# Second attention: half of its output normed and turned inside the loop, and gate products issued a step ahead

## The reference

```python
def diff_attention(q, k, v, lam):               # 8 heads, each with 2 maps of 64 channels
    ...
        s = jnp.einsum('bqhmd,bkhmd->bhmqk', qblk, k) * (HEAD_DIM ** -0.5)
        p = jax.nn.softmax(s, axis=-1)
        p = p[:, :, 0] - lam * p[:, :, 1]
        return jnp.einsum('bhqk,bkhe->bqhe', p, v)
    ...
def token_mixer(h, ...):
    z_hy, q, k, v, gates = jnp.split(h @ w_in, SPLITS, axis=-1)
    y_hy = hyena_branch(...) @ w_hy_out
    ...                                          # 256 own keys and 256 context keys
    o = diff_attention(q, k, v, lam)
    o = rmsnorm_2(o, subln_g) * (1.0 - lam_init) # over the 128 channels of one head
    y_da = o.reshape(B, L, D_ATTN) @ w_da_out
    g_hy, g_da = jnp.split(jax.nn.sigmoid(gates), 2, axis=-1)
    return (g_hy * y_hy + g_da * y_da) @ w_o
```

## Time and profile before

| | |
|---|---|
| median of 3 runs | 2538.65 us |
| profiled execution, its own time | 2539.34 us |
| its span (first to last instruction) | 2537.5 us |
| PE busy | 2464.7 us, 97% |
| DVE busy | 1777.1 us, 70% |
| ACT busy | 1448.3 us, 57% |
| chain that ended last | PE 89%, DVE 6%, ACT 2%, issue 1%, DMA 1% |
| the attention loop with its tail | 2194.27 to 2302.31 us from the span's start |

### The profile page before, as it was taken

The page is one execution under the profiler, slowest core; times in us unless marked ns, Lnnn a source line. Parts: engine busy times, 40 slices in busy tenths (PEclk is TensorE's granted clock), DMA queues, the critical chain, the costliest instruction groups (busy, mean ns, idle before and its releaser), DMA issues.

```text
span 2537.5 us, 32448 instructions
## 1 busy us (share of the span) xinstructions
PE 2464.7 (97%) x11675; PEld 1970.2 (78%) x11675; DVE 1777.1 (70%) x1662; ACT 1448.3 (57%) x1571; POOL 92.8 (4%) x76
## 2 busy tenths in 40 slices
PE   8999999989999999999999999999999999998999
PEld 6578887667788888888888887888884697677887
DVE  6464546668888898889888986655443578777554
ACT  4454344456777777777777775445442344466443
POOL 0000000012000000000000000410000000000000
PEclk9899999999999999999999999999999999998999
DMA  6867663768999999999999997665543354335651
GB/s 222 288 232 239 213 213 108 265 222 310 390 394 374 390 371 387 368 394 367 390 374 382 372 350 269 230 203 182 182 165 108 113 171 150 123 98 176 213 186 66
DMA packets 333407, 650.29 MB, mean 256 GB/s; under 512 B 14856, under 2 KB 113736, under 8 KB 333128
## 3 DMA queue, kind: packets, MB, share of 16 engines
q1 hardware_dynamic: 327992, 630.73, 70.5%
q0 software_dynamic: 5232, 18.38, 1.8%
q10 hardware_dynamic: 96, 0.02, 0.0%
HBM read 634.91 MB, written 14.17 MB: 256 GB/s over the span
## 4 chain that ended last, share of the span: by engine, by line
PE 89%; DVE 6%; ACT 2%; issue 1%; DMA 1%; SPq 0%; POOL 0%; DVEq 0%; ACTq 0%; POOLq 0%
PE ps L961 23%; PE ps L874 20%; PE ps L1001 11%; PE ps L916 10%; PE ps L806 5%; PE ps L1355 5%; PE ps L1385 2%; PE ps L1287 2%; DVE ringL L2424 1%; PE ps L1092 1%; PE ps L986 1%; PE ps L849 1%; PE ps L887 1%; PE ps L1504 1%; DVE As L2454 1%
## 5 line engine op out<-in xcount | busy, mean ns | idle before, releaser
L2454 DVE TENSOR_TENSOR As<-ringA,As 128x2048 fp32r<-128x2048 f32 x316 | 728.5, 2306 | 205.8 <-ACT As L1714 108.2
L961 PE MATMUL ps<-As,xgs 128*128 128x512 f32 x2688 | 648.6, 394 | 8.2 <-DVE As L2454 5.9
L961 PEld LDWEIGHTS ps<-As,xgs 128*128 128x128 f32 x2688 | 501.8, 189 | 113.5 <-issue 6.2
L1803 ACT ACTIVATE As<-ringA 128x2048 fp32r<-128x2048 f32 x224 | 429.0, 1915 | 100.1 <-PE ps L961 94.9
L874 PE MATMUL ps<-As,xs 128*128 128x512 f32 x1408 | 363.2, 395 | 0.0
L1001 PE MATMUL ps<-Bs,hds 128*128 128x512 f32 x1320 | 318.5, 390 | 1.8 <-DVE hds L2525 1.4
L874 PEld LDWEIGHTS ps<-As,xs 128*128 128x128 f32 x1408 | 262.0, 188 | 56.4
L1001 PEld LDWEIGHTS ps<-Bs,hds 128*128 128x128 f32 x1320 | 247.0, 188 | 55.5 <-issue 4.3
L2544 DVE TENSOR_TENSOR Bs<-ringB,Bs 128x2048 fp32r<-128x2048 f32 x110 | 251.8, 2289 | 18.1 <-ACT Bs L1842 17.8
L916 PE MATMUL ps<-Bs,hds 128*128 128x512 f32 x1056 | 248.0, 390 | 0.1
L1842 ACT ACTIVATE Bs<-ringB 128x2048 fp32r<-128x2048 f32 x110 | 211.4, 1922 | 59.0 <-PE ps L1001 58.1
(11 more groups left out here) (436 smaller groups left out, 3185.7 us busy)
## 6 DMA issues: line engine op xcount, KB each, us to landing
ringB<-in_moe_w_down SPq DMA_DIRECT2D x112, 1024.0 KB, 7.3
ringA<-in_moe_w_gate SPq DMA_DIRECT2D x112, 1024.0 KB, 7.4
ringA<-in_moe_w_up SPq DMA_DIRECT2D x112, 1024.0 KB, 7.0
ringA<-in_w_ff_in SPq DMA_DIRECT2D x132, 512.0 KB, 4.6
ringA<-in_w_in SPq DMA_DIRECT2D x56, 1024.0 KB, 5.3
ringA<-in_w_ada SPq DMA_DIRECT2D x36, 1024.0 KB, 6.9
ringB<-in_w_ff_out SPq DMA_DIRECT2D x33, 1024.0 KB, 4.9
ringA<-in_dense_w_gate SPq DMA_DIRECT2D x28, 512.0 KB, 3.5
```

The lines of the kernel that those rows point to most:

```text
L961: m = mm(ps[:, bank, :], lhs(l, tt, k), As[:, h, r, k % 4, :], start=k == 0 and n == 0, stop=k == KC - 1 and n == 2)
L1803: A(As[:, h, 0, :, :], ringA[:, (p["a"] + u) % 2, 4 * h:4 * h + 4, :], ACT.Copy).then_inc(A_high, 1)
L2454: V.tensor_tensor(As[:, h, 1, :, :], ringA[:, (p["a"] + u) % 2, 4 * h:4 * h + 4, :], f32(As[:, h, 0, :, :]), ALU.subtract).then_inc(A_spli ...
```

## The change

Nothing is added to or taken from the arithmetic on PE. Six things move.

1. PE issues `gates_part(0)` ahead of the loop and `gates_part(n + 1)` at the head of step n. The splits of the gates' weights on ACT and DVE stay in their steps, but for one ACT copy ahead of the loop (second half of block 0), which now stands among the copies of the turned q and k.
2. Norm of heads 0 to 3 in the loop: two table loads and a small square root on ACT in step 9, a reciprocal and two scalings of 512 columns on DVE at the end of step 10 (`heads_scaled(0)`).
3. `turn_out` of heads 0 to 3 goes into PE's step 14, to banks 4 and 5; their split stands behind the loop on DVE and in step 15 on ACT.
4. DVE's `weight_low` for the first half of "dao" moves from behind the loop to the end of step 14, ahead of the softmax arithmetic of step 15.
5. Heads 4 to 7 are normed, and then turned by PE between the first and the second of the products of block 0.
6. On DVE the `weight_low` of the second half of "dao" goes ahead of the split of heads 4 to 7.

```diff
+            def turn_out(src, at, hf):
+                for tt in range(TILES):
+                    if at == 0:
+                        pe.wait_ge(o_scaled, 2 * hf + tt + 1)
+                    ...
             scores(0)
             scores(1)
+            gates_part(0)
             for n in range(NU):
                 h = n // 2
-                gates_part(n)
+                if n + 1 < NU:
+                    gates_part(n + 1)
                 pe.wait_ge(s2_p, n + 1)
...
                 if n + 2 < NU:
                     scores(n + 2)
+                elif n + 2 == NU:
+                    turn_out(O2, 0, 0)
                 pe.wait_ge(s2_pt, n + 1)
...
-            pe.wait_ge(s2_o, NU)
-            pe.wait_ge(pj_act, ph["gt2"]["ja"] + 8)
-            for hf in range(2):
-                turn_out(O2, 0, hf)
             p = ph["dao"]
...
                     for tt in range(TILES):
+                        if n == 0 and h == 0 and tt == 1:
+                            pe.wait_ge(s2_o, NU)
+                            pe.wait_ge(pj_act, ph["gt2"]["ja"] + 8)
+                            turn_out(O2, 0, 1)
                         if n == 0:
                             pe.wait_ge(ot_lo, 2 * h + tt + 1)
...
@@ ScalarE
-                late_high(*nxt, 1)
+                if nm != "hyo" or n == 0:
+                    late_high(*nxt, 1)
             for i in range(0, 12, 2):
+                if i == 4:
+                    late_high(ph["gt2"], 0, 1)
...
+                if n == 15:
+                    out_high(0, 0, scale=small[:, 257:258])
...
-                if n:
+                if n == 9:
+                    nc.scalar.preload_act_table(ACT.Sqrt)
+                    ch.done(head_square(8))
+                    head_roots(0)
+                    nc.scalar.preload_act_table(ACT.Exp)
+                elif n:
                     head_square(n - 1)
...
@@ VectorE
+            def heads_scaled(hf):
+                dve.wait_ge(s2_o, 8 * hf + 8)
+                dve.wait_ge(sl_std, hf + 1)
+                ...
+                ch.done(V.reciprocal(to, of))
+                for tt in range(TILES):
+                    ...
+                    V.tensor_tensor(o4, o4, to[:, tt, :].unsqueeze(2).broadcast_to([P, 4, P]), ALU.mult).then_inc(o_scaled, 1)
...
                 if n < 14:
                     rowmax(n + 2)
-            weight_low(ph["dao"], 0, 0)
+                if n == 10:
+                    heads_scaled(0)
+                if n == 14:
+                    weight_low(ph["dao"], 0, 0)
+            out_low(0, 0, small[:, 257:258])
             gather_out(15)
...
+            heads_scaled(1)
...
-            for hf in range(2):
-                out_low(0, hf, small[:, 257:258])
             weight_low(ph["dao"], 0, 1)
+            out_low(0, 1, small[:, 257:258])
```

More of the change, by code:

```diff
@@ L420, in build, with ot_bank @@
         LATE_BANK = {("q2", 0): 0, ("q2", 1): 2, ("kv2", 0): 2, ("kv2", 1): 4, ("kv2", 2): 0, ("kv2", 3): 2, ("hyo", 0): 6, ("hyo", 1): 4}
+        def ot_bank(at, hf, tt):
+            return 4 + tt if at == 0 and hf == 0 else 2 * hf + tt
         def back(c):
@@ L1488, in _ @@
             NU = 16
+            def turn_out(src, at, hf):
+                for tt in range(TILES):
+                    if at == 0:
+                        pe.wait_ge(o_scaled, 2 * hf + tt + 1)
+                    for j in range(4):
+                        last = tr(ps[:, ot_bank(at, hf, tt), j * P:(j + 1) * P], src[:, tt, (4 * hf + j) * P:(4 * hf + j + 1) * P], ident)
+                    last.then_inc(ot_tp, 1)
             scores(0)
             scores(1)
+            gates_part(0)
             for n in range(NU):
                 h = n // 2
-                gates_part(n)
+                if n + 1 < NU:
+                    gates_part(n + 1)
                 pe.wait_ge(s2_p, n + 1)
@@ L2257, in head_square, with out_high, head_roots @@
                 return A(fnrow[:, n % 8 * P:(n % 8 + 1) * P], O2[:, tt, h * P:(h + 1) * P], ACT.Square, accum_out=small[:, 416 + 8 * tt + h:417 + 8 * tt + h])
+            def out_high(at, hf, **kw):
+                for tt in range(TILES):
+                    act.wait_ge(ot_tp, at + 2 * hf + tt + 1)
+                    A(hcTR[:, 4 * hf:4 * hf + 4, tt * P:(tt + 1) * P], ps[:, ot_bank(at, hf, tt), :].rearrange("p (k n) -> p k n", k=4), ACT.Copy, **kw).then_inc(ot_hi, 1)
+            def head_roots(hf):
+                at, to = (small[:, o:o + 16].rearrange("p (t h) -> p t h", t=TILES)[:, :, 4 * hf:4 * hf + 4] for o in (416, 432))
+                A(to, at, ACT.Sqrt, scale=1.0 / P, bias=epsc[1e-6]).then_inc(sl_std, 1)
             weigh(0)
@@ L2277, in _ @@
             ch.done(head_square(15))
-            A(small[:, 432:448], small[:, 416:432], ACT.Sqrt, scale=1.0 / P, bias=epsc[1e-6]).then_inc(sl_std, 1)
+            head_roots(1)
             late_high(ph["dao"], 0, 1)
[L2281 to L2285, removed]
-            for hf in range(2):
-                out_high(0, hf, scale=small[:, 257:258])
+            out_high(0, 1, scale=small[:, 257:258])
             act.wait_ge(pj_act, ph["gt2"]["ja"] + 8)
@@ L3167, in gather_out, with out_low @@
                 V.tensor_copy(O2[:, tt, h * P:(h + 1) * P], ps[:, 0, 0:P]).then_inc(s2_o, 1)
+            def out_low(at, hf, gain=None):
+                for tt in range(TILES):
+                    dve.wait_ge(ot_hi, at + 2 * hf + tt + 1)
+                    dst = (slice(None), slice(4 * hf, 4 * hf + 4), slice(tt * P, (tt + 1) * P))
+                    src = ps[:, ot_bank(at, hf, tt), :].rearrange("p (k n) -> p k n", k=4)
+                    if gain is None:
+                        V.tensor_tensor(hTR[dst], src, f32(hcTR[dst]), ALU.subtract).then_inc(ot_lo, 1)
+                    else:
+                        V.scalar_tensor_tensor(hTR[dst], src, gain, f32(hcTR[dst]), ALU.mult, ALU.subtract).then_inc(ot_lo, 1)
+            def heads_scaled(hf):
+                dve.wait_ge(s2_o, 8 * hf + 8)
+                dve.wait_ge(sl_std, hf + 1)
+                to, of = (small[:, o:o + 16].rearrange("p (t h) -> p t h", t=TILES)[:, :, 4 * hf:4 * hf + 4] for o in (416, 432))
+                ch.done(V.reciprocal(to, of))
+                for tt in range(TILES):
+                    o4 = O2[:, tt, 512 * hf:512 * hf + 512].rearrange("p (h d) -> p h d", d=P)
+                    V.tensor_tensor(o4, o4, to[:, tt, :].unsqueeze(2).broadcast_to([P, 4, P]), ALU.mult).then_inc(o_scaled, 1)
             rowmax(0)
@@ L3186, in _ @@
                     rowmax(n + 2)
-            weight_low(ph["dao"], 0, 0)
-            gather_out(15)
[L3189 to L3205, removed]
+                if n == 10:
[3 more added lines that the diff above has]
+            out_low(0, 0, small[:, 257:258])
+            gather_out(15)
+            heads_scaled(1)
             def mix(n, tt):
```

## The result

| | before | changed |
|---|---|---|
| median | 2535.07 us (6 runs, 2529.11 to 2543.61) | 2578.45 us (6 runs, 2570.63 to 2587.07) |
| profiled execution | 2539.34 us, span 2537.5 | 2587.07 us, span 2585.3 |
| ratio to before | | 1.017, 95% interval 1.0151 to 1.019 |

The change makes the kernel slower by 43.4 us on the medians; 2580 was forecast, in a range of 2566 to 2596. The profiled execution of the changed kernel is the slowest of its six, and its first gate product comes 6.58 us later than before (2200.85 against 2194.27), behind code that is all but the same. So that part of the difference between the two profiled executions is not shown to be the change's. Over the nine traces of this study that point lies anywhere between 2186.24 and 2200.85.

The account below looks back on a forecast made before the run. TensorE (PE), busy 97% of the span, was taken as the bound. Terms -3.8 + 28.0 + 1.6 + 1.7 = +27.5 us at full clock, plus 14 for the clock, gave +41.5 on 2539.34: forecast 2580, range 2566 to 2596.

Parts of the forecast that it names:

- Start: Step 0: the second gate part fills PE's 2.10 us wait and the clock should not fall; -3.8 us.
- Six waits: Steps 3, 4, 7, 8, 11, 12: PE waits 4.67 us each for DVE's split of a weight half; +28.0 us.
- 28 to 30: Sign: idle time before the first gate products of parts 4, 5, 8, 9, 12, 13, ended by `ringL`, us in all.
- Head norm in the loop: Norm of heads 0 to 3: DVE's reciprocal and scalings count in full, +1.6 us; ACT's table loads cost 0.
- Clock: Half clock behind seven new waits, six in the loop and one at step 15: 2.0 us each, +14.
- Rival 1: The clock stays at 1.00 behind the waits, so only +27.5 us: 2567; chance 0.08.
- rival 2: The clock is low in every burst, pairs of waits run wholly at 0.50: 2596; chance 0.15.
- PE's busy time: Sign: growth by much less than 10 us or more than 25 would show the clock forecast wrong.
- Tail: From step 14's transposes (S) to the second "dao" block: S + 25.2 against 23.45, +1.7 us, from -2 to +4.
- forecast wait of 4.5 us: PE at the transposes of step 15 waits for the softmax, behind DVE's "dao" split, where 3.38 us went.
- rival 3: Not slower: the weight halves are ready when PE wants them, the six waits do not occur: 2533; chance 0.04.
- rival 4: The waits move but a later stage absorbs them: 2539; chance 0.03.

Follow-up runs that it names:

- filled waits: Changed kernel with 34 products of 256 columns, whose results nobody reads, in front of each of the six waits: ratio 1.0112 to before.
- splits put ahead: Changed kernel with the gates' weight splits on ACT and DVE moved a step ahead as well: ratio 0.9993 to before.
- root in a gap: Changed kernel with weight splits a step ahead, table loads and root moved from step 9 to 12, head scaling to step 13: ratio 0.9972 to before.

## Why the prediction was right

**Start.** Predicted -3.8. From the first gate product to the transposes of step 1 the kernel before took 12.15 us (2194.27 to 2206.42), the changed one 10.97 (2200.85 to 2211.82) with one gate part of 2.85 more inside: -4.0. No idle time stands ahead of step 0's transposes, and the clock is 1.00 over these 10.97 us.

**Six waits.** Predicted 6 x 4.67 and 1.6 for the head scaling, 29.6 us. The six waits and the one at step 10's value products sum to 28.1 us in the trace. The chain of 10.02 us a step is shown twice, by the filled waits (10.01 to 10.06) and by the splits put ahead, which remove it. The measured idle time (4.41, 4.50) is below 4.67 because a record of PE ends about 0.2 us behind the start of the next one. For the same reason, and because 2.10 us of the fifth wait are ended by ACT, the six waits ended by `ringL` sum to 26.0 us and not to the 28 to 30 that I had named as a sign.

**Head norm in the loop.** I had the table loads hidden and the scaling exposed by 1.6. The fifth wait shows both: 2.10 us for ACT's copy and 3.78 for the split, 5.88 against 4.50 in the kernel with gate parts ahead only, 1.4 us more. The scaling makes that difference: from `rowmax` to the end of the split DVE took 6.85 us (2288.57 to 2295.42) against 5.40 in step 7. The value products that the loads held up ended at about 2291.8, and DVE took them up only later, without a wait:

```profile
2292.94 0.28 DVE L3189 COPY arena<-ps 128x128 f32<-128x128 f32 x1
```

The two loads took 1.28 us each with the next instruction at once behind them:

```profile
2286.15 1.28 ACT L2293 ACT_TABLE_LOAD   x1
2287.44 0.31 ACT L2268 ACTIVATE fnrow<-arena 128x128 f32<-128x128 f32 x1
...
2287.88 0.30 ACT L2278 ACTIVATE small<-small 128x8 f32<-128x8 f32 x1
2288.19 1.28 ACT L2296 ACT_TABLE_LOAD   x1
2289.49 0.60 ACT L2303 ACTIVATE arena<-ps 128x512 f32<-128x512 f32 x1
2289.98 0.59 ACT L2285 ACTIVATE arena<-ps 128x512 f32<-128x512 f32 x1
```

The copy L2285 starts at 2289.98, 2.5 us later than 0.62 us behind the transposes of step 10 (2286.86), where 2.45 was forecast. There is no drain of 1380 ns such as the Trainium skill gives (ScalarE: Activation LUTs, What ACT_TABLE_LOAD costs); here the measurement decides, and its 1283 ns for the load itself agrees.

**Clock.** Predicted 2.0 us a wait. The six steps took 12.50, 12.01, 12.40, 11.38, 13.02 and 12.44 us, 41.65 more than six of 5.35; less the predicted 29.6 at full clock, 12.0 are the clock, 2.0 a wait. The filled waits show the size without that forecast: the five steps other than the fifth took 60.73 us in the changed kernel and 50.21 with the waits filled, 2.1 us a wait. Rival 1 (the clock holds, 2567) and rival 2 (low in every burst, 2596) are both out: over 5.8 to 6.6 us behind the six waits the granted clock was 0.54 to 0.76. Rival 2 came nearest behind the first and the sixth, where the first 5.35 us ran wholly at 0.50, but over all the waits of the loop the fall cost 12 us, not 29.

PE's busy time, another of my signs, grew by 11.6 us in the section (101.18 to 112.73), inside the 10 to 25 named. Over the whole trace it grew by 21.6, of which 9.0 lie ahead of the section, so the page alone is a poor witness for it.

**Tail.** Predicted: from the transposes of step 14, S + 25.2 against 23.45, with 2 us of clock beside it. Measured: 26.02 (2323.05 to 2349.07), so +2.6, against 3.7 for the two together. PE ran at 0.50 from 2330.04 to 2336.04, but what ended the stretch was DVE's last split, only 0.8 us later than S + 25.2; so the clock term of 2.0 was too large here. The forecast wait of 4.5 us at the transposes of step 15 is the 4.55 in the rows. The chain behind it is as worked out: split, softmax, `out_high`, load and root, scaling, turn, and a last wait of 2.14 for the split behind the sigmoid chain:

```profile
2326.12 2.29 DVE L2446 TENSOR_TENSOR ringL<-ringA,ringH 128x2048 fp32r<-128x2048 f32 x1 [3.51 <-ACT ringH L1702]
...
2336.11 1.29 DVE L3209 TENSOR_TENSOR arena<-arena,small 128x512 f32<-128x512 f32 x2
...
2342.95 2.29 DVE L3246 TENSOR_TENSOR arena<-arena,xn 128x2048 f32<-128x2048 f32 x1 [1.73 <-ACT xn L2313]
...
2346.72 2.29 DVE L2446 TENSOR_TENSOR ringL<-ringA,ringH 128x2048 fp32r<-128x2048 f32 x1 [1.48 <-ACT ringH L1702]
```

**What the sum left out.** Behind the wait of 2.14 us the clock fell once more (0.62 from 2349 to 2353), so the stretch from the second "dao" block to the first product of the next feed-forward took 41.24 us (2349.07 to 2390.31) against 39.48 (2302.31 to 2341.79): +1.8 us that I had in no term. The same stretch took 39.61 to 39.65 us in three kernels whose clock stood at 1.00 behind their shorter wait there (norm and tail edits alone, splits ahead, root in a gap), and 41.22 with the waits filled, where it fell to 0.57. -4.0 + 41.65 + 2.6 + 1.8 = 42.05 us, against a forecast of 41.5 and 43.4 between the medians. The last 1.4 us I cannot place; they are within what the runs vary. That the sum came so near is in part luck: the tail with its clock came out 1.1 us under its forecast, and the 1.8 us that no term had made up for it.

Rivals 3 and 4 are out, but my argument against rival 3 named the wrong tie. I had `gather_out(n - 1)` hold the split back, since it waits for PE's value products. In the rows of step 7 these ended at about 2255.1 and `gather_out` started at 2257.00 without a wait, so it held nothing back. What kept DVE from being early is `rowmax`, which stands ahead of it in the order and waited 2.15 us for PE's scores (2254.08). Against rival 4: nothing behind the loop gave the time back.

## What to carry to other kernels

Moving a consumer a step ahead moves every hand-over that it waits for; if the producer on the other engine keeps its place, a chain that lay beside the work becomes part of the cycle. Before such a move, read one steady step in the timeline and measure from when the last input was ready to when it was used: here 0.7 us of slack against a move of one step, 5.35 us. Work that is put into a busy loop belongs in the step, and at the place in it, where its engine stands idle; the same loads and scalings cost 3.75 us in step 10, with the half clock behind their wait, and nothing in steps 12 and 13.

## What the runs showed of the hardware

The clock's answer to a wait is not fixed. A wait of 2.10 us at the same instruction, behind more than 50 us of uninterrupted work, was followed by full clock in one kernel (1.00 over the next 4.63 us) and by half clock in another (0.65 over the next 4.92, costing 1.65 us). Each kernel has one trace, so it stays open whether the kernel or the single execution decided. At the second "dao" block, waits of 1.92 and 1.93 us were followed by 1.00 over the next 4 us in three kernels, and waits of 2.11 and 2.14 us by 0.57 and 0.62 in two. Behind five of the six waits, those of 4.4 to 4.5 us, the fall cost 1.3 to 2.5 us each (a step of the changed kernel less the same step with the wait filled). So an estimate of the clock's share holds for a sum of several waits, not for one.
